# Gated-delta chunk chain: the state meets the raw keys, and the triangular inverse acts on the sum

## The reference, cut to what matters

```
a_mat = (kb k^T) * decay_strict + I          # unit lower triangular, per chunk
u = solve(a_mat, v * beta)
w = solve(a_mat, kb * exp(g))
for each chunk:
    v_new = u - w S
    o     = qg S + qk v_new
    S     = S * exp(g_last) + kd^T v_new
```

## Time and profile before

| | us |
|---|---|
| runs of the kernel | 1780.74, 1786.04, 1789.45; median 1786.04 |
| span of the profiled execution, first to last instruction | 1776.4 |
| median less span (start and end of a run outside the span; the profiled execution has no separate time) | 9.6 |
| PE busy over the span | 1482.2 (83%) |
| DVE, ACT, POOL busy | 612.1, 496.5, 411.5 |
| the gated-delta heads, from the first L705 to the end of the last L791 | about 79 to 546 |
| starts of L761 in heads 0 to 7 | 128.6, 190.0, 251.3, 319.3, 380.6, 432.8, 484.9, 533.1 |

### The profile page before, as it was taken

How to read it: one execution, slowest core, us unless ns; L and a number is a source line. 1 busy time by engine, 2 the same in 40 slices (tenths; PEclk the granted TensorE clock), 3 DMA queues, 4 the chain that set the end, 5 groups by cost and what they waited for, 6 DMA issues and landing times. The chain is left out here.

```text
span 1776.4 us, 25676 instructions
## 1 busy us (share of the span) xinstructions
PE 1482.2 (83%) x9233; PEld 1033.1 (58%) x9233; DVE 612.1 (34%) x1230; ACT 496.5 (28%) x1124; POOL 411.5 (23%) x566
## 2 busy tenths in 40 slices
PE   4999998899988877887773699999999967888871
PEld 2877776778764544444441687788874544544440
DVE  3655544556542434111102512223232435111114
ACT  4324333333331111111122344444442101111123
POOL 3312202202220022323221243333310012332321
PEclk8899999999999778989996599999999959999996
DMA  8254354430143248999897111111115419999984
GB/s 355 84 190 169 142 187 168 146 140 1 48 201 119 107 170 367 425 423 421 362 401 289 51 48 48 48 48 47 54 76 237 154 61 390 394 423 422 419 360 191
DMA packets 52446, 372.44 MB, mean 210 GB/s; under 512 B 12920, under 2 KB 13392, under 8 KB 24720
## 3 DMA queue, kind: packets, MB, share of 16 engines
q1 hardware_dynamic: 40128, 354.51, 49.7%
q0 software_dynamic: 12160, 16.83, 2.6%
q10 hardware_dynamic: 80, 0.04, 0.0%
HBM read 366.55 MB, written 27.83 MB: 222 GB/s over the span
## 5 line engine op out<-in xcount | busy, mean ns | idle before, releaser
L1090 ACT COPY arena<-PS 128x128 f32<-128x128 f32 (+2 forms) x356 | 168.1, 482 | 641.9 <-PE PS L888 236.9
L881 PE MATMUL PS<-Wr,arena 128*64 128x256 f32 x2368 | 287.2, 397 | 30.5 <-DVE arena L1814 21.2
L881 PEld LDWEIGHTS PS<-Wr,arena 128*64 128x64 f32 x2368 | 190.1, 145 | 150.6 <-issue 57.1
L888 PE MATMUL PS<-Dr,arena 128*64 128x512 f32 x512 | 141.5, 677 | 65.1 <-DMA Dr<-in_moe_w_down_dram 37.1
L653 PE MATMUL PS<-hHi,Whi 128*128 128x512 f32 x384 | 176.3, 459 | 3.7 <-issue 3.1
L2054 POOL DMA_INDIRECT y_rows<-arena x74 | 75.7, 1022 | 336.9 <-ACT arena L1090 319.9
L655 PE MATMUL PS<-hHi,Wlo 128*128 128x512 f32 x384 | 153.3, 399 | 0.0
L654 PE MATMUL PS<-hLo,Whi 128*128 128x512 f32 x384 | 152.9, 398 | 0.0
L1995 POOL TENSOR_TENSOR Wlo<-Wr,Whi 128x512 fp32r<-128x512 f32 (+1 forms) x80 | 104.5, 1320 | 201.4 <-ACT Whi L1090 201.4
L1820 DVE TENSOR_TENSOR arena<-arena,PS 128x128 f32<-128x128 f32 x64 | 18.4, 287 | 378.4 <-ACT arena L1295 378.3
L888 PEld LDWEIGHTS PS<-Dr,arena 128*64 128x64 f32 x512 | 35.0, 143 | 118.5 <-issue 99.1
(11 more groups left out here) (311 smaller groups left out, 2398.4 us busy)
## 6 DMA issues: line engine op xcount, KB each, us to landing
Wr<-in_moe_w_gate_up_dram SPq DMA_DIRECT2D x74, 2048.0 KB, 17.4
Dr<-in_moe_w_down_dram SPq DMA_DIRECT2D x64, 1024.0 KB, 13.4
Dr<-in_ada_w_dram SPq DMA_DIRECT2D x42, 1024.0 KB, 6.3
Wr<-in_gdn_w_dram SPq DMA_DIRECT2D x8, 2048.0 KB, 8.3
Wr<-in_fox_w_dram SPq DMA_DIRECT2D x8, 2048.0 KB, 8.0
Wr<-in_moe_w_down_dram SPq DMA_DIRECT2D x10, 1024.0 KB, 13.2
arena<-y_rows SPq DMA_DIRECT2D x16, 512.0 KB, 6.7
X<-in_x_dram SPq DMA_DIRECT2D x2, 2048.0 KB, 10.4
```

Of the source, the lines that this page charges most:

```text
L881: last = mm(out_bank[C * g:C * g + C, 0:DE], at, w[:, k, g * DE:g * DE + DE], start=(k == 0), stop=(k == KD - 1))
L888: last = mm(out_bank[C * g:C * g + C, :], act_t[:, C * k:C * k + C], w[:, k * D + g * 512:k * D + g * 512 + 512], start=(k == 0), stop=(k ...
L1090: return nc.scalar.copy(dst, src)
```

## The change

`kwn` and `nWT` go away: no product of the inverse with the keys for all chunks, no ACT copy of it, no DVE multiplication by minus beta e^g. Instead POOL copies the next keys, before they are transposed, to a tile of their own, `kT`; in the chain PE multiplies `kT` by S into PSUM bank 4, DVE scales that by minus beta e^g and adds it to the chunk's part of `vb`, and only then PE applies `XiT`. The units between the links are placed anew: one unit after the keys meet the state and one after `XiT`, one after the state's matmul of chunk 0, and none after the state's matmuls of chunks 1 and 2, nor after the last output.

```diff
--- PE, delta
-                for n in range(NT):
-                    last = mm(tile(PS[4], n), tile(kwn, n), tile(XiT, n), start=True, stop=True)
-                last.then_inc(wt_ps, 1)
+                units = iter((24, 25, 26, 27, 28, 28, 29, 30, 30, 31, 32))
+                at = next(units)
                 for n in range(NT):
                     if n == 0:
                         pe.wait_ge(vb_ok, d + 1)
-                    last = mm(PS[5][:, 0:P], tile(XiT, n), tile(vb, n), start=True, stop=(n == 0))
-                    if n > 0:
+                    else:
                         if n == 1:
-                            pe.wait_ge(wt_ok, d + 1)
+                            pe.wait_ge(kt_ok, d + 1)
                         pe.wait_ge(s_ok, d * 3 + n)
-                        last = mm(PS[5][:, 0:P], tile(nWT, n), S, start=False, stop=True)
-                    last.then_inc(vn_ps, 1)
-                    fill(24 + 2 * n, 25 + 2 * n)
+                        mm(tile(PS[4], n), tile(kT, n), S, start=True, stop=True).then_inc(ks_ps, 1)
+                        mm(tile(PS[7], n), S, tile(qg, n), start=True, stop=False)
+                        to = next(units)
+                        fill(at, to)
+                        at = to
+                        pe.wait_ge(tk_ok, d * 3 + n)
+                    mm(PS[5][:, 0:P], tile(XiT, n), tile(vb, n), start=True, stop=True).then_inc(vn_ps, 1)
+                    to = next(units)
+                    fill(at, to)
+                    at = to
                     if n == 0:
                         after(pe, ot_ok, d)
                         pe.wait_ge(qg_ok, d + 1)
-                    else:
-                        mm(tile(PS[7], n), S, tile(qg, n), start=True, stop=False)
                     pe.wait_ge(vn_ok, d * 4 + (n + 1))
                     last = mm(tile(PS[7], n), vnew[:, n % 2, :], tile(qkT, n), start=(n == 0), stop=True)
                     if n < NT - 1:
                         last = mm(PS[6][:, 0:P], tile(kdec_k, n), vnew[:, n % 2, :], start=True, stop=True)
                         last.then_inc(s_ps, 1)
+                        to = next(units)
+                        fill(at, to)
+                        at = to
                     else:
                         last.then_inc(o_ps, 1)
-                    fill(25 + 2 * n, 26 + 2 * n)
--- ACT, delta
-                act.wait_ge(wt_ps, d + 1)
-                cp(nWT, PS[4][:]).then_inc(wt_ok, 1)
                 take(2)
--- DVE, delta
-                TT(t4(kwn), t4(PS[3][:]), hcol(nbeg, d), ALU.mult)
                 TT(t4(kdec_k), t4(PS[3][:]), over(kdk), ALU.mult).then_inc(kd_ok, 1)
...
                     if s is not None and l in (5, 6):
+                        if l == 5:
+                            dve.wait_ge(kt_ok, d + 1)
                         conv(s, 1, (2 * l - 10, 2 * l - 9))
...
                         STT(out=S, in0=S, scalar=egl[:, ds(d * NT + n, 1)], in1=PS[6][:, 0:P],
                             op0=ALU.mult, op1=ALU.add).then_inc(s_ok, 1)
+                    ahead = vb[:, (n + 1) * P:(n + 2) * P]
+                    dve.wait_ge(ks_ps, d * 3 + (n + 1))
+                    STT(out=ahead, in0=PS[4][:, (n + 1) * P:(n + 2) * P], scalar=nbeg[:, ds(d * NT + (n + 1), 1)], in1=ahead,
+                        op0=ALU.mult, op1=ALU.add).then_inc(tk_ok, 1)
                     if s is not None:
                         conv(s, 2, ((0, 1), (2,), (3,))[n])
--- POOL, delta
                 if s is not None:
                     head_rows(s)
+                pool.wait_ge(sq_ok, d * 2 + 1)
+                after(pool, ks_ps, d * 3)
+                passed()
+                g.tensor_copy(kT, qkv[1]).then_inc(kt_ok, 1)
                 pool.wait_ge(at_ok, d + 1)
```

More of the change, by code:

```diff
@@ L218, in build @@
         qg, qkT, aT, Xi = cv(T), cv(T), cv(T), cv(T)
-        vb, kwn, kdec_k = cv(T), cv(T), cv(T)
+        vb, kT, kdec_k = cv(T), cv(T), cv(T)
         XiT, Pp = cv(T), cv(T)
@@ L226, in build @@
         ssk, lnk, rk, irk, rb, bj, kdk = (cv(NT) for _ in range(7))
-        nWT = aT
         gate_s = [shiftB[:, 0:T], shiftB[:, T:2 * T]]
@@ L325, in build @@
         nt_ok, x1_ps, x1_ok, p_ps, p_ok, lv_ps, lv_ok = (sem(n) for n in ("nt_ok", "x1_ps", "x1_ok", "p_ps", "p_ok", "lv_ps", "lv_ok"))
-        wt_ps, wt_ok, vn_ps, vn_ok, s_ps, s_ok = (sem(n) for n in ("wt_ps", "wt_ok", "vn_ps", "vn_ok", "s_ps", "s_ok"))
+        ks_ps, kt_ok, tk_ok, vn_ps, vn_ok, s_ps, s_ok = (sem(n) for n in ("ks_ps", "kt_ok", "tk_ok", "vn_ps", "vn_ok", "s_ps", "s_ok"))
         o_ps, osq_ok, osum_ok, sso_ps, ro_ok, ot_ok = (sem(n) for n in ("o_ps", "osq_ok", "osum_ok", "sso_ps", "ro_ok", "ot_ok"))
```

## The result

The changed kernel takes 1796.29 us (median of 4 runs, 1795.32 to 1797.46), the kernel before 1785.23 (4 runs, 1780.74 to 1789.45): ratio 1.0058, interval 1.0040 to 1.0077, so slower by 7 to 14 us, most likely 10. Forecast was 1793.2, range 1785 to 1799. In absolute time 1796.29 is 3 us above the forecast; against the kernel before, the loss is 10 us where 7.1 was forecast.

A forecast was written before the change was run, and what follows sets the result against it. The prediction took each head's chain up to its last output as the bound, with PE's work behind it free. Loop heads +0.99, heads 0, 5, 6 +0.85, head 7 +0.63 made +7.1 us: 1793.2, range 1785 to 1799.

The forecast's parts named there:

- The path: End of each head: the last output sets the next head's start; PE's work behind it is free, 1.56 us over.
- The first chunk: Chain's start: L761 and one ACT copy leave, L781 comes after about 1.2 us, not 2.57; gain 1.35 a head.
- The last head: Head 7, without units: from L761 to its last L781 10.12 us instead of 9.49, so +0.63.
- The crossings: Chunks 1 to 3: DVE's step 0.96 us against 1.14 of PE work, vnew 0.94 against 0.92; taken at nothing.
- the state's term: After chunks 1 and 2: PE waits for the new S; +0.12 us twice in loop heads, +0.05 twice outside.
- What costs nothing: L1608 leaving DVE gains 0 to 0.1 us; POOL's copy of the keys, 0.71 us, lies in idle time.
- rival 1: Crossings to DVE and vnew don't fit below PE's units: slower by over 0.5%, 1795 to 1798; chance 0.27.
- rival 3: Removed work counts in full and waits for S do not appear: 1786 to 1790; chance 0.16.
- rival 2: PE's longer idle time ahead of L709 lowers its clock at each front: 1816 us; chance 0.07.
- The sum: All heads: 4 x 0.99 + 3 x 0.85 + 0.63 = +7.1 us on 1786.04, so 1793.2.
- My main forecast: Whole kernel slower by +4 to +8.9 us, 8.9 being the 0.5% limit of what can be told; chance 0.50.

The follow-up runs named there:

- its front filled: Changed kernel with nine unused 128x128 identity matmuls in PE's idle time ahead of L708: 1798.10 us, ratio 1.0076.
- its last unit behind: Changed kernel with unit 31 moved from ahead of the last output to behind it: 1795.52 us, ratio 1.0067.
- its units at the old marks: Changed kernel with one unit behind XiT by vb, one behind the state's matmul, none behind keys by S, the last behind the last output: 1792.32 us, ratio 1.0045.
- its DMA issue behind the vnew: Changed kernel with ACT's DMA issue of the conditioning rows moved behind the first vnew, PE waiting itself for their sums: 1795.46 us, ratio 1.0047.
- both: Changed kernel with the units at the old marks and ACT's DMA issue behind the first vnew: 1792.25 us, ratio 1.0034.
- before, unit ahead: Kernel before with its last unit moved from behind the last output to ahead of it: 1789.39 us, ratio 1.0009.
- before, ACT's order: Kernel before with ACT's first vnew ahead of the copy of negative W and the DMA issue: 1778.34 us, ratio 0.9952.

## Why the prediction was right, and where it was short

**The path.** That the last output sets the next head's start held in every profile: with a unit behind that output the front waits 1.56 us, without it 2.25, and the output-to-front distance stays (3.56, before 3.54; 3.64 where the last output's matmul starts from a wait). The reasons for a loss held too: a unit more ahead of the last output, and 16 waits of PE for the new S.

**The first chunk.** Here a term was mis-sized: I gave 1.2 us to the first output's matmul for all heads. Heads 5 and 6 have 1.20; heads 0 to 4 have 1.30, 1.60, 1.52, 1.59, 1.53, about 1.5 us together more than forecast. I had looked at ACT's two copies and had not counted the DMA issue that stands between the product's copy and the vnew in these heads. Before, it lay under the copies; with one copy gone it became what the vnew waited for. The run with the issue behind the vnew shows it (1.27 in heads 1 to 4). From the first output on, the loop heads took 9.97 to 10.01 us where the forecast had 9.96.

**The last head.** Forecast +0.63, measured +1.17. A link from XiT to the output's matmul took 1.19 where I had 1.08; keys by S to XiT took 0.94 in chunks 2 and 3 where I had 0.84. Both L769 and L775 start from a wait there, and I had counted no restart.

**The crossings.** The new DVE step fitted below its unit in heads 0 to 6, as taken: L775 waits for it in the last head alone. From a delayed L769 to L775 PE needs 1.25 us rather than 1.14, which is the restart of 0.08 to 0.1 that I had put into the state's term. From L785 to the next L769 it is 0.95 in the loop and 0.89 outside, forecast 0.96 and 0.89.

**What costs nothing.** POOL's copy takes 0.61 us and starts right at the front:

```profile
207.30 0.61 POOL L2026 COPY arena<-arena 128x512 f32<-128x512 f32 x1 [1.75 <-ACT arena L1248]
```

DVE has no instruction beside it in any of the eight heads. L723 waited for DVE no longer than before where it waited (0.44 to 0.48 in the loop's heads). The removal of L1608 shows nowhere in the chain.

**The rivals.** The crossings (rival 1) gave the right side, slower by over 0.5%, and a band in which the measured time lies (1795 to 1798), but not the mechanism: the wait at XiT that it asks for is absent in heads 0 to 6. Removed work in full without the waits (rival 3) is out: PE waits for the new S 16 times, and the ratio is clear of 1. The clock (rival 2) fell at three fronts in the changed kernel's profile. I had argued against it from one window with a wait of 2.5 us (L724 of head 7, for DVE), behind which the granted clock stayed at 1.00. That execution was luck: in the second profile of the same code the same wait, 2.47 us, is followed by a fall to the lower level, 1.2 GHz (first line the first profile, second line the second):

```profile
507.00:510.00 3.00, 2.33 (x14) 1.53 (x14) 3.00 (x8) 1.13 (x2) 3.00 (x3) 1.00 1.08 452
514.00:517.00 3.00, 2.33 (x11) 1.93 (x10) 3.00 (x7) 0.58 (x1) 3.00 (x3) 0.50 1.10 464
```

The falls cost about 1 us at each of two fronts and nothing at the third, not the 3.3 a front that I had priced. They did not decide: with the fronts filled the time did not come down.

**The sum.** 9.6 us of chain against 7 to 14 measured. Set side by side for all kernels, against the kernel before (the intervals are those of the ratios):

| kernel | chains of the 8 heads, us | time, us | interval |
|---|---|---|---|
| changed | +9.6 | +10.4 | 7.1 to 13.7 |
| its front filled | +9.6 | +13.6 | 9.3 to 17.9 |
| its last unit behind | +8.8 | +12.0 | 8.6 to 15.4 |
| its units at the old marks | +6.4 | +8.0 | 5.2 to 10.9 |
| its DMA issue behind the vnew | +8.3 | +8.4 | 5.5 to 11.4 |
| both | +5.1 | +6.1 | 3.8 to 8.6 |
| before, unit ahead | +5.3 | +1.6 | -1.1 to 4.3 |
| before, ACT's order | -5.6 | -8.6 | -11.6 to -5.5 |

In seven of eight the chain's difference lies in the interval of the time; the kernel before with its unit ahead is the exception, and why is open. So the chain is enough for the result, but that a microsecond of chain is a microsecond of time is shown only as closely as this table does. The mean granted clock of each execution is on record too: over the 62 later executions of the kernel before the time goes with it, 1.3 us more for each 0.001 of clock less (0.909 to 0.919), and the changed kernel's four stand at 0.912 to 0.913. At the same clock the line through those 62 leaves about 7.5 us between the two kernels (an estimate), so some 3 of the 10 us go along with the lower clock, whether as its effect or as a sign of the same idle times.

My main forecast, +4 to +8.9 us with a chance of 0.50, did not come true; what came is slower by over 0.5%, to which I had given 0.34. The point forecast was closer in absolute time than its terms deserve: the first chunk was short by 1.5 us and the last head by 0.5, both to the same side.

## What to carry to other kernels

When filler work is placed by hand, count what lies ahead of the event that others wait for; filler behind it leaves the chain alone up to that wait's length, and a serial crossing added ahead of it lengthens the chain even if its engine work is less. How much of that the time shows has to be measured: one such move of 5.3 us showed at most 4.3. When an instruction leaves an engine's stream, look at what stands next to it there, a DMA issue too: it had been covered by what goes. The chain's first gap, which this change partly closed, was worth more by reordering ACT alone (-0.5%) than by the new algebra.

## What the runs showed of the hardware that I had not expected

Two executions of the same code had spans of 1776.4 and 1790.8 us with identical chains; what differed in the heads (9.6 us) were the falls of TensorE's granted clock (one and four) and one more wait of 1.3 us for a DMA in two heads. The fall behind a 2.5 us wait of PE came in one and not in the other. Filling PE's idle time at one place removed the falls there; in that profile they stood at others, and there was no gain.

A DMA issued by ACT took 0.53 us of its instruction stream, from 256.10 to 256.63, and delayed a 0.37 us instruction behind it by about 0.3, while the copy ahead of it was still running. In the kernel before the same issue (0.54 us from 191.40) ended ahead of the second copy's end, and the first output's matmul comes at 2.57 to 2.58 us with it and without it.
